# A two-model transformer forward pass on one core: the activations of all weight products move 16 bytes in SBUF

## The chip, the cores and the metric

The kernel runs on one core of a Trainium2 chip. The metric is the device time of one execution in microseconds (us), the median of a few runs. Three runs of the kernel before gave 2869.03, 2871.64 and 2883.26 us.

## The reference

Two small transformers run one after the other on a sequence of 256 tokens of 1024 features, in float32. The first has two layers of feed-forward, a mixer with four branches (a causal convolution, a short convolution, sliding-window attention, forgetting attention) and another feed-forward. The second has four layers of a mixer (differential attention, a gated recurrence, a gated unit, differential attention again), an attention over a memory of 256 tokens, and a feed-forward. Cut to what matters here:

```python
def _swiglu(x, w_gate, w_up, w_down):
    return (jax.nn.silu(x @ w_gate) * (x @ w_up)) @ w_down

for l in range(DEPTH):                       # DEPTH = 2
    x = x + 0.5 * _swiglu(_rmsnorm(x, ffn1_norm[l]), ...)
    z = _rmsnorm(x, mix_norm[l]) @ w_in[l]   # 1024 -> 6660 columns
    ...                                      # four branches, each @ its own 256 x 1024 matrix
    x = x + merged @ w_out[l]
    x = x + 0.5 * _swiglu(_rmsnorm(x, ffn2_norm[l]), ...)
for i in range(DEPTH_2):                     # DEPTH_2 = 4
    x = x + mix
    x = x + mem_cross_attention(rmsnorm(x, norm_cross[i]), mem_n, ...)
    x = x + swiglu(rmsnorm(x, norm_ffn[i]), ffn_w_gu[i], ffn_w_down[i])
return rmsnorm(x, norm_final)
```

Nearly all arithmetic is the product of 256 tokens with weight matrices of 1024 by 1024 or by 2816.

## The kernel before

**Weights.** They are cut into units of 128 partitions by 2048 float32 values (1 MB). A ring of five slots in SBUF, `raw`, takes them in from HBM in order, issued by SyncE (line 385). ScalarE rounds each unit to the reduced form float32r as its high part `wh` (line 1113), and GpSimd writes the rest, `wl` = `raw` - `wh`, over `raw` (line 400). VectorE and ScalarE do the same with activations: `ah` and `al` for the normalized input, `gh` and `gl` for the gated values of a feed-forward, `mh` and `ml`, `oh` and `ol`, `hoh` and `hol`, `soh` and `sol` in the other stages.

**A product.** TensorE adds three matmuls for each pair of tiles, high by low, low by high and high by high (`product`, lines 454 to 456). Each has a stationary operand of 128x128 and a moving operand of 128x256. In `features` the weights are stationary and the activations move; in `tokens` it is the other way round. A unit is 16 pairs, so 48 matmuls. A feed-forward stage of 33 units is 1584 matmuls.

**Order.** The order of the work on each engine is written out by hand, and semaphores tie the engines together: a unit's slot is loaded again when TensorE has signalled `unit_done`, and TensorE waits on `low_ready` before a unit. Where a stage has small attention products or a softmax, these stand between the units on TensorE.

**Addresses.** What the change touches is where things lie in SBUF. All tensors are placed by hand, with a running offset `at[0]` per partition. `sb` places a tensor at the offset and steps it by the width rounded up to 32 bytes; `w` places one inside the work area, and these names share it, stage by stage. The weights (`raw`, `wl`, `wh`) begin at a multiple of 64 bytes, and their slots are 8192 bytes apart. After them and `x` the code skips 192 bytes, and pads the work area to the same place:

```python
at[0] += 192
acts_at = at[0]
...
at[0] += (raw_at + 192 - at[0]) % 256
work_at = at[0]
```

So `ah`, `al`, `full`, `mh`, `ml` and all high and low parts in the work area start 192 bytes, modulo 256, after the start of the weights. Within each tensor a product's slice begins at a multiple of 512 bytes. `decays` (a part of the constants `con`) is multiplied with `lh` and `ll` in lines 934 and 935; they start at the same place modulo 256. `ident`, the identity that transposes use, is the first part of `con`, and lies there too, as do `vc` (keys and values of the memory), `pt2` and `prob2`.

Of the kernel before, what the change touches and what calls it, by code (L numbers as in the profile page):

```python
# [18 lines left out]
F32 = mybir.dt.float32  # L19
F32R = mybir.dt.float32r  # L20
# [5 lines left out]
P = 128  # L26
T = 256
TB = T // P
D = 1024
KD = D // P  # L30
# [98 lines left out]
def build(nc, w_units, params_d, consts_d, hot_d, rel_d, x_d, mem_d, ws_d, bs_d, out_d,  # L129
          table_d, units=UNITS, stop_after=None):  # L130

    at = [nc.sbuf_base]

    def sb(name, width, dt=F32, offset=None):

        if offset is None:
            offset = at[0]
            at[0] += (4 * width + 31) // 32 * 32
        return nc.alloc_sbuf_tensor_at(name, [P, width], dt, offset=offset)

    at[0] = (at[0] + 63) // 64 * 64
    raw_at = at[0]
    raw = sb("raw", RING * UW)
    wl = sb("wl", RING * UW, F32R, offset=at[0] - 4 * RING * UW)
    wh = sb("wh", RING * UW, F32R)
    x = sb("x", KD * T)
    at[0] += 192
    acts_at = at[0]
    ah = sb("ah", KD * T, F32R)
    al = sb("al", KD * T, F32R)  # L150
    full = sb("full", KD * T)
    mh = sb("mh", KD * T, F32R)
    ml = sb("ml", KD * T, F32R)
    par = sb("par", NPAR)
    con_at = at[0]
    con = sb("con", NCONST)
# [5 lines left out]
    at[0] += (raw_at + 192 - at[0]) % 256  # L162
    work_at = at[0]
    WORK = 12288
    work = sb("work", WORK)
    assert at[0] <= nc.sbuf_usable_end, (at[0], nc.sbuf_usable_end)

    def w(name, first, width, dt=F32):
        assert first + width <= WORK
        return sb(name, width, dt, offset=work_at + 4 * first)  # L170

    gh = w("gh", 0, FP * 512, F32R)
    gl = w("gl", FP * 512, FP * 512, F32R)

    up = w("up", 0, 2 * (CK - 1 + T))
    acc = w("acc", 576, 512)
    sp = w("sp", 1088, 2 * (SK - 1 + T))
# [2706 lines left out]
def program(nc, arrays, **kw):  # L2884
    args = [nc.dram_tensor(k, list(a.shape), F32, kind="ExternalInput").ap() for k, a in arrays.items()]
    args.append(nc.dram_tensor("out", [P, KD * T], F32, kind="ExternalOutput").ap())
    args.append(nc.dram_tensor("tables", [12, P, PERIOD], F32, kind="Internal").ap())
    build(nc, *args, **kw)
# [12 lines left out]
```

How the kernel before makes its waits and increments, by code:

```python
        @block.sync  # L365
# [8 lines left out]
                sp.dma_start(raw[:, n * UW:(n + 1) * UW], w_units[n, :, :]).then_inc(raw_landed[n], 16)  # L374
                if n == 1:
                    sp.dma_start(onehot[0:NB + 1, :], hot_d).then_inc(tables_in, 16)
                    sp.dma_start(rel[0:NB + 1, 0:12], rel_d).then_inc(tables_in, 16)
            sp.dma_start(par[:, KD:NPAR], params_d[:, KD:NPAR]).then_inc(par_rest, 16)
            sp.dma_start(con[:, :], consts_d).then_inc(consts_in, 16)
            with sp.Fori(1, units // RING) as i:
                for j in range(RING):
                    sp.wait_ge(unit_done, RING * i + (j + 1 - RING))
                    sp.dma_start(raw[:, j * UW:(j + 1) * UW], w_units[i * RING + j, :, :])\
                        .then_inc(raw_landed[j], 16)
            for c2 in range(KD // 2):
                sp.wait_ge(result, c2 + 1)
                sp.dma_start(out_d[:, 512 * c2:512 * (c2 + 1)], full[:, 512 * c2:512 * (c2 + 1)])\
                    .then_inc(stored, 16)
            sp.wait_ge(stored, 16 * (KD // 2))
# [2 lines left out]
        @block.gpsimd  # L395
# [1 line left out]
            def low(n, j):  # L397
                pool.wait_ge(high_ready, n + 1)
                pool.tensor_tensor(wl[:, j * UW:(j + 1) * UW], raw[:, j * UW:(j + 1) * UW],
                                   wh[:, j * UW:(j + 1) * UW].bitcast(F32), ALU.subtract)\
                    .then_inc(low_ready, 1)
            pool.wait_ge(low_ready, 2)
            for j in range(2, RING):
                low(j, j)
```

## Time and profile before

| what | value |
|---|---|
| runs | 2869.03, 2871.64, 2883.26 us; median 2871.64 |
| profiled execution, span | 2878.8 us (7.2 us above the median, inside the runs' range) |
| TensorE busy | 2822.3 us, 98% of the span |
| ScalarE, VectorE, GpSimd busy | 46%, 37%, 73% |
| weights moved | 459 loads of 1 MB and 4 of 256 KB |
| mean granted TensorE clock | 0.989 |

The profiled execution's own time is given by its span, from the first to the last instruction. Busy time of TensorE is no measure of its pace: matmuls are pipelined, so one is still under way when the next begins. Its pace is the distance between starts. The granted clock is the share of TensorE's full 2.4 GHz; 0.5 is the lower level of 1.2 GHz.

### The profile page before, as it was taken

Reading aid. Unit: us, or ns where it says so; the run is one execution under the profiler, and the core shown is the slowest. Engines: PE = TensorE matmul, PEld = TensorE weight load, DVE = VectorE, ACT = ScalarE, POOL = GpSimd, SP = SyncE. Lnnn points to the kernel's source line nnn. Section 1 sums busy time; section 2 is a strip of 40 time slices with the busy share of each in tenths; the row PEclk is TensorE's granted clock in tenths of the full one; section 3 lists DMA queues with packets and bytes.
Section 4 is the critical chain, followed back from the end, with each engine's and each line's share of the span. In section 5 each row is a group of like instructions: output and inputs, shape, how many; then the busy total and the mean of one; then the engine's idle time right before and its main releaser. Section 6 shows DMA issues by size and latency. Waiting matters only on the chain.

```text
span 2878.8 us, 55910 instructions
## 1 busy us (share of the span) xinstructions
PE 2822.3 (98%) x24180; PEld 2771.7 (96%) x24180; DVE 1066.5 (37%) x1865; ACT 1333.4 (46%) x1490; POOL 2108.9 (73%) x462
## 2 busy tenths in 40 slices
PE   8999999999999999999999999999999999999998
PEld 8999889999999899999999998999999999999998
DVE  4217534213155443445333144333123331453331
ACT  5335544344355454345443484444354443454442
POOL 6777657878876578776768783659886688767785
PEclk9999999999999899999999999999999999999999
DMA  7974344555554355554445542445554455544553
GB/s 231 193 198 170 135 144 176 191 185 188 199 184 152 112 192 189 182 185 147 168 169 191 191 177 87 158 144 197 191 204 153 147 195 196 191 147 161 176 192 116
DMA packets 74197, 496.88 MB, mean 173 GB/s; under 512 B 8399, under 2 KB 13135, under 8 KB 14968
## 3 DMA queue, kind: packets, MB, share of 16 engines
q1 hardware_dynamic: 68344, 485.88, 46.9%
q10 hardware_dynamic: 5632, 7.62, 2.7%
q8 instruction: 191, 3.13, 0.4%
q14 instruction: 30, 0.25, 0.0%
HBM read 490.05 MB, written 3.41 MB: 171 GB/s over the span
## 4 chain that ended last, share of the span: by engine, by line
PE 86%; POOL 4%; DMA 3%; issue 3%; DVE 2%; ACT 2%; ACTq 0%; SPq 0%; POOLq 0%; DVEq 0%
PE G L454 21%; PE G L456 21%; PE G L455 21%; PE S L454 5%; PE S L456 5%; PE S L455 5%; POOL wl L400 4%; DMA raw<-w_units 2%; PE G L691 1%; PE S L1042 1%; ACT wh L1113 1%; DMA bias<-tables 0%; PE S L842 0%; PE S L799 0%; PE S L805 0%
## 5 line engine op out<-in xcount | busy, mean ns | idle before, releaser
L400 POOL TENSOR_TENSOR wl<-raw,wh 128x2048 fp32r<-128x2048 f32 x458 | 2108.7, 4616 | 740.5 <-ACT wh L1113 719.0
L1113 ACT ACTIVATE wh<-raw 128x2048 fp32r<-128x2048 f32 x456 | 873.7, 1918 | 1045.6 <-DMA raw<-w_units 1045.5
L454 PE MATMUL G<-ah,wl 128*128 128x256 f32 x4304 | 1209.2, 281 | 15.6 <-DVE wl L1768 8.9
L455 PE MATMUL G<-al,wh 128*128 128x256 f32 x4304 | 1200.6, 279 | 0.0
L456 PE MATMUL G<-ah,wh 128*128 128x256 f32 x4304 | 1200.3, 279 | 0.0
L454 PEld LDWEIGHTS G<-ah,wl 128*128 128x128 f32 x4304 | 816.4, 190 | 24.1 <-issue 15.1
L455 PEld LDWEIGHTS G<-al,wh 128*128 128x128 f32 x4304 | 815.2, 189 | 0.6
L456 PEld LDWEIGHTS G<-ah,wh 128*128 128x128 f32 x4304 | 814.1, 189 | 0.0
L454 PE MATMUL S<-gh,wl 128*128 128x256 f32 x1408 | 391.4, 278 | 3.4 <-POOL wl L400 3.4
L455 PE MATMUL S<-gl,wh 128*128 128x256 f32 x1408 | 391.3, 278 | 0.0
L456 PE MATMUL S<-gh,wh 128*128 128x256 f32 x1408 | 391.2, 278 | 0.0
L454 PEld LDWEIGHTS S<-gh,wl 128*128 128x128 f32 x1408 | 265.0, 188 | 3.7 <-issue 3.7
L456 PEld LDWEIGHTS S<-gh,wh 128*128 128x128 f32 x1408 | 265.1, 188 | 0.0
L455 PEld LDWEIGHTS S<-gl,wh 128*128 128x128 f32 x1408 | 265.1, 188 | 0.0
L1921 DVE TENSOR_TENSOR G<-G,root 128x512 f32<-128x512 f32 x88 | 61.5, 698 | 361.3 <-PE G L456 361.3
L1959 DVE SCALAR_TENSOR_TENSOR S<-S,x 128x512 f32<-128x512 f32 x28 | 19.6, 700 | 367.1 <-PE S L456 365.9
L1919 DVE TENSOR_TENSOR G<-G,root 128x512 f32<-128x512 f32 x88 | 61.4, 698 | 184.4 <-PE G L456 184.1
L454 PE MATMUL G<-mh,wl 128*128 128x256 f32 x384 | 108.3, 282 | 3.3 <-DVE ml L2120 2.8
L454 PE MATMUL G<-wh,al 128*128 128x256 f32 x384 | 108.0, 281 | 0.8 <-DVE ll L2563 0.8
L455 PE MATMUL G<-wl,ah 128*128 128x256 f32 x384 | 107.2, 279 | 0.0
L456 PE MATMUL G<-wh,ah 128*128 128x256 f32 x384 | 107.1, 279 | 0.0
L456 PE MATMUL G<-mh,wh 128*128 128x256 f32 x384 | 106.9, 279 | 0.0
(371 smaller groups left out, 3786.3 us busy)
## 6 DMA issues: line engine op xcount, KB each, us to landing
raw<-w_units SPq DMA_DIRECT2D x459, 1024.0 KB, 4.8
bias<-tables ACTq DMA_DIRECT2D x24, 128.0 KB, 3.2
tables<-trow ACTq DMA_DIRECT2D x12, 192.0 KB, 9.0
con<-consts SPq DMA_DIRECT2D x1, 1056.0 KB, 16.8
x<-x_in SPq DMA_DIRECT2D x4, 256.0 KB, 5.8
raw<-w_units SPq DMA_DIRECT2D x4, 256.0 KB, 6.9
memx<-mem_in ACTq DMA_DIRECT2D x1, 1024.0 KB, 7.4
out<-full SPq DMA_DIRECT2D x4, 256.0 KB, 2.5
```

Of the source, the lines that this page charges most:

```text
L400: pool.tensor_tensor(wl[:, j * UW:(j + 1) * UW], raw[:, j * UW:(j + 1) * UW], wh[:, j * UW:(j + 1) * UW].bitcast(F32), ALU.subtract)\
L454: pe.matmul(out, sl, vh, start=start and k == 0, stop=False, **kw)
L455: pe.matmul(out, sh, vl, start=False, stop=False, **kw)
L456: ins = pe.matmul(out, sh, vh, start=False, stop=stop and k == len(parts) - 1, **kw)
L691: ins = pe.matmul(out, v_of(kc), pt[:, kc * 512 + n * P:kc * 512 + (n + 1) * P], start=kc == 0, stop=kc == nk // P - 1)
L1042: ins = pe.matmul(out[:, h * T:(h + 1) * T], qf[:, f * T + g * P:f * T + (g + 1) * P], kc[:, f * T:(f + 1) * T], start=dc == 0, stop=dc == 1)
L1113: act.activation(wh[:, j * UW:(j + 1) * UW], raw[:, j * UW:(j + 1) * UW], ACT.Copy)\
L1919: dve.tensor_tensor(pairs(gate), pairs(gate), along, ALU.mult).then_inc(scaled, 1)
L1921: dve.tensor_tensor(pairs(value), pairs(value), along, ALU.mult).then_inc(up_scaled, 1)
L1959: dve.scalar_tensor_tensor(xs if last else held[k], held[k], factor, xs, ALU.mult, ALU.add)\
```

## The change

Activations that enter products with weights get a helper of their own, `behind`. It places a tensor that is 4 values (16 bytes) wider at the old offset and returns the part behind these 4 values. `ah`, `al`, `full`, `mh`, `ml` and everything that `w` places in the work area now start 16 bytes further. The parameters and constants (`par`, `con` with `ident` and `decays`, `ones`, `root`, `small`) start 32 bytes further; the work area's own start stays, because the padding before it takes this up, and `merged`, `pb`, `kc`, `vc`, `memx`, `memn` and `comp` behind it start 32 bytes further. `decayed` stays. The weights and `x` stay. No instruction, wait or transfer is added, removed or put elsewhere in the order of its engine.

Modulo 256, the distance from weights to activations goes from 192 to 208. The distance from `lh` to `decays` goes from 0 to 16, that from `pt2` to `vc` and from `prob2` to `ident` too.

```diff
@@ -138,19 +138,28 @@
+    def behind(name, width, dt=F32, offset=None):
+
+        if offset is None:
+            offset = at[0]
+            at[0] += 4 * width
+        return nc.alloc_sbuf_tensor_at(name, [P, SKEW + width], dt, offset=offset)[:, SKEW:SKEW + width]
+
     at[0] = (at[0] + 63) // 64 * 64
     raw_at = at[0]
+    SKEW = 4
...
     at[0] += 192
     acts_at = at[0]
-    ah = sb("ah", KD * T, F32R)
-    al = sb("al", KD * T, F32R)
-    full = sb("full", KD * T)
-    mh = sb("mh", KD * T, F32R)
-    ml = sb("ml", KD * T, F32R)
+    ah = behind("ah", KD * T, F32R)
+    al = behind("al", KD * T, F32R)
+    full = behind("full", KD * T)
+    mh = behind("mh", KD * T, F32R)
+    ml = behind("ml", KD * T, F32R)
+    at[0] += 32
     par = sb("par", NPAR)
...
-    work = sb("work", WORK)
+    work = sb("work", WORK + 2 * SKEW)
...
     def w(name, first, width, dt=F32):
         assert first + width <= WORK
-        return sb(name, width, dt, offset=work_at + 4 * first)
+        return behind(name, width, dt, offset=work_at + 4 * first)
```

## Rows read from the trace of the kernel before

**Rows 1.** page: busy time of each engine; the chain that ended last, by engine

```profile
PE 2822.3 (98%) x24180; PEld 2771.7 (96%) x24180; DVE 1066.5 (37%) x1865; ACT 1333.4 (46%) x1490; POOL 2108.9 (73%) x462
...
PE 86%; POOL 4%; DMA 3%; issue 3%; DVE 2%; ACT 2%; ACTq 0%; SPq 0%; POOLq 0%; DVEq 0%
```

**Rows 2.** groups by line and shape: count | busy us, mean ns | idle before

```profile
L400 POOL TENSOR_TENSOR wl<-raw,wh 128x2048 fp32r<-128x2048 f32 x458 | 2108.7, 4616 | 740.5 <-ACT wh L1113 719.0 <-ACT wh L1142 20.9
L454 PE MATMUL G<-ah,wl 128*128 128x256 f32 x4304 | 1209.2, 281 | 15.6 <-DVE wl L1768 8.9 <-DVE wl L1800 3.4 <-DVE merged L2178 3.2
...
L1113 ACT ACTIVATE wh<-raw 128x2048 fp32r<-128x2048 f32 x456 | 873.7, 1918 | 1045.6 <-DMA raw<-w_units 1045.5
...
L454 PE MATMUL S<-gh,wl 128*128 128x256 f32 x1408 | 391.4, 278 | 3.4 <-POOL wl L400 3.4
...
L454 PE MATMUL G<-mh,wl 128*128 128x256 f32 x384 | 108.3, 282 | 3.3 <-DVE ml L2120 2.8 <-DVE logf L2655 0.5
L454 PE MATMUL G<-wh,al 128*128 128x256 f32 x384 | 108.0, 281 | 0.8 <-DVE ll L2563 0.8
...
L454 PE MATMUL G<-oh,wl 128*128 128x256 f32 x384 | 106.5, 277 | 0.0
...
L454 PE MATMUL G<-wh,ml 128*128 128x256 f32 x256 | 72.2, 282 | 0.0
...
L454 PE MATMUL S<-mh,wl 128*128 128x256 f32 x128 | 35.9, 280 | 1.5 <-issue 1.5
...
L454 PE MATMUL G<-soh,wl 128*128 128x256 f32 x64 | 19.5, 304 | 4.2 <-ACT kc L1238 4.2
...
L454 PE MATMUL G<-hoh,wl 128*128 128x256 f32 x64 | 17.8, 278 | 0.0
```

**Rows 3.** slower stretches: us A:B, length, PE busy (matmuls), granted clock, DMA share, GB/s

```profile
36.30:176.80 140.50, 140.50 (x1196) 1.00 0.90 201
...
463.70:646.60 182.90, 182.90 (x1555) 1.00 0.52 186
...
1720.50:1742.50 22.00, 22.00 (x189) 1.00 0.47 168
...
sum 854.40, PE 854.40; mean PE 38.84
```

**Rows 4.** faster stretches, the same view

```profile
1480.30:1658.60 178.30, 178.30 (x1576) 1.00 0.55 195
...
2697.30:2864.60 167.30, 167.30 (x1479) 1.00 0.48 170
sum 1266.70, PE 1266.70; mean PE 74.51
```

**Rows 5.** TensorE in order of time: start us, us, instruction, out<-moving,stationary

```profile
1742.68 0.29 PE L934 MATMUL S<-decays,lh 128*128 128x256 f32 x1
...
1744.36 0.28 PE L934 MATMUL S<-decays,lh 128*128 128x256 f32 x1
```

**Rows 6.** the same view, merged rows of float32 matmuls

```profile
1436.34 1.47 PE L1054 MATMUL G<-con,prob 128*128 128x128 f32 x12
...
1438.67 7.31 PE L691 MATMUL G<-pt,vc 128*128 128x128 f32 x64
```

**Rows 7.** line 2044, the convolution: duration ns min/median/max, starts, forms

```profile
L2044 DVE SCALAR_TENSOR_TENSOR S<-up,par,S x116: 480/485/493, 233.7 to 884.4; 128x256 f32<-128x256 f32 x116
```

**Rows 8.** page: loads of bias; chain of waits: start us, us, what

```profile
bias<-tables ACTq DMA_DIRECT2D x24, 128.0 KB, 3.2
...
1260.57 7.92 DMA bias<-tables
...
2481.02 6.29 DMA bias<-tables
```

## Prediction

> **What bounds the kernel now.** I read the page's shares first. TensorE is busy for 98% of the span and holds 86% of the chain that ended last; every other engine stands far below [rows 1]. Then the groups of instructions: the sums of the products with weights stand in lines 454 to 456, three matmuls for each pair of operands (low weights by high activations, high by low, high by high). Line 454 alone has 4304 + 1408 + 384 + 384 + 384 + 256 + 128 + 64 + 64 = 7376 of them [rows 2]. Times three that is 22128 products of 128x128 by 128x256, out of 24180 matmuls. The column of mean durations (some 280 ns) is no help, because matmuls overlap. What counts is the spacing from start to start, so the third view is the table by stretches: time of a stretch divided by the matmuls in it.
>
> That table shows something that no mean shows. In any long stretch without a wait the products come at one of two spacings. In 22 stretches, 854.4 us together, it is 117.8 ns: 182.9 us for 1555 matmuls gives 117.6, and 140.5 for 1196 gives 117.5 (one more start than gaps at an edge; at the third decimal it is 117.8) [rows 3]. In 17 others, 1266.7 us together, it is 113.3 ns: 178.3 us for 1576 and 167.3 for 1479 give 113.1 [rows 4]. The granted clock is 1.00 in all of them, the upper level of 2.4 GHz, so the clock is not what differs. Nor is it the work: 463.7 to 646.6 and 1480.3 to 1658.6 are the same kind of stage, a feed-forward of 1584 products, and the first takes about 4.6 us more for it. The spacing is set when the stage begins and then stays. 256 columns at 2.4 GHz are 106.7 ns, so each product loses 6.6 or 11.1 ns.
>
> What could take it? In the stream, the load of the next stationary operand runs beside the matmul, so two reads of SBUF run together: 1024 bytes per partition of the moving operand and 512 of the stationary one. All slices in the products are multiples of 512 bytes within their tensors, so each pair stands at one distance modulo 256: activations less weights is 192. Where the activations are the stationary operand it is 64 the other way round; the stretch from 1720.5 us is of that kind and has 117.8 ns too [rows 3]. One pair of the program stands at distance 0, `decays` and `lh`: there the steady spacing is 1.68 us for 14 gaps, from 1742.68 to 1744.36, or 120.0 ns [rows 5]. So the distance matters, or at least the three spacings differ with it at one clock; 0 is the worst seen, and 192 sits between two states. Other matmuls, of 128 columns and plain float32, come closer: 12 transposes in 1.47 us are (1.47 - 0.27) / 11 = 109.1 ns apart, and 64 of `pt` by `vc` in 7.31 us are 111.7 [rows 6]. They are not the same operation, and serve as a lower bound only.
>
> **The change, part by part.** No instruction is added, removed or moved on any engine; waits and queues are the same. Only addresses change.
>
> - Products by the 192 distance go to 208, those the other way round from 64 to 48. This is the only term that can be large: each nanosecond on 22128 products is 22 us. The trace has no row at 208. The nearest rows bound it: from above 120.0 ns (distance 0) [rows 5], from below 109.1 ns (the nearest matmul that keeps its full rate) [rows 6]. The present time in these terms: the slow stretches hold 854.4 / 0.1178 = 7253 products, the fast ones 1266.7 / 0.1133 = 11180; 3695 are left in short stretches, and split alike (39% slow) they make it 8700 slow and 13430 fast. The value I take is 113.3 ns for all. Two steady spacings at one distance look to me like a place at the edge of a good region, where one more or one less clash of the two reads fits into a product; 16 bytes can move it inside. That saves 8700 x 4.45 ns = 39 us. The other side is as simple: out of the region, everything at 117.8 costs 13430 x 4.45 = 60 us, everything at 120.0 costs 13430 x 6.67 + 8700 x 2.2 = 109 us.
> - `decays` by `lh` and `ll` (128 matmuls) goes from 0 to 16 bytes, since the constants move 32 and the others 16. Between 109.1 and 120.0 ns for 128 of them it is at most 1.4 us of gain, and I take 0. The float32 products of the attention (`pt`, `vc`, `prob` by the identity) go from 0 to 16 bytes apart. Besides the 22128 products and these 128 there are 1924 matmuls of all kinds, so 5 ns on each (more than the step between the two kinds in [rows 6]) would be 10 us either way. I take 0.
> - VectorE, ScalarE and GpSimd now read and write from 16 bytes past a multiple of 64. The row of the convolution's taps shows VectorE indifferent: `up` is read at 30 starting points 4 bytes apart, and 116 instructions take 480 to 493 ns [rows 7]. I take 0. ScalarE and GpSimd have no such row; both have idle time (46% and 73% busy) [rows 1], GpSimd's work on the weights lies between tensors that don't move, and a unit of 48 products at 113.3 ns (5.44 us) still covers its 4.62 us and ScalarE's 1.92 us [rows 2]. Even at 109.1 ns the unit is 5.24 us, so neither becomes the bound.
> - DMAs into `bias1`, `bias2`, `swt` and `sbs`, and those out of `full`, now start at 16 bytes past a multiple of 32. 24 loads of bias take 3.2 us at the median, and the longest pieces of the chain hold two of them, 7.92 and 6.29 us [rows 8]. If these two doubled it would be 14 us; a gain has no reason. I take 0, and 14 for the upper end.
>
> The sum: 2878.8 - 39 = 2839.8 us against the profiled execution. That span is 7.2 us above the runs' median of 2871.64, and inside their range (2869.03 to 2883.26), so the forecast for the median is 2833 us, or 1.3% less.
>
> At one place a rule speaks against this. The Trainium skill, page "TensorE: Matmul & The Clock Gate", section on what happens when a matmul is issued, says that TensorE has two independent read ports into SBUF and that loading the next weights takes nothing from the running matmul. The same page, in the section on 56 against 53.3 ns, gives 2.5 ns over the columns' time, which would be 109.2 ns here. By that the distance could not matter. The rows don't fit it: 113.3, 117.8 and 120.0 ns at one clock. But if the port rule holds and the spacing comes from something else that is set at a stage's start, the change does nothing but deal the spacings anew; that is the second rival.
>
> **The rivals.**
>
> 1. Toward the bad distance. 208 is nearer to 256, and 48 nearer to 0, than 192 and 64 were, and 0 is where 120.0 ns stands. The price is that of one more stall in each product: all at 117.8 ns gives 2872 + 60 = 2932 us, all at 120.0 gives 2981. It decides from the point where the mean spacing passes 115.1 ns, today's mean ((8700 x 117.8 + 13430 x 113.3) / 22130). For it: the only measured point on that side is the worst one, and the two read streams drift past each other once in each 256 bytes, so a step of 16 may just as well add a meeting. Against it: 16 bytes of 64 is a short way, and the state at 113.3 ns already holds most of the time.
> 2. Nothing but a new deal. The distance is not what sets the spacing, or 208 has the same two states. The state taken on by a single feed-forward stage is worth 1584 x 4.45 ns = 7 us, and the runs' own range is 14 us wide; the sum then lies within 2872 +- 14 us. For it: the same distance shows both spacings in the same kind of stage. Against it: distance 0 has a third spacing that neither stretch shows.
> 3. Clear of it altogether. All products at 111.7 ns would give 2833 - 22128 x 1.6 ns = 2798 us, at 109.1 ns 2740 us. For it: other matmuls do this in the same program [rows 6]. Against it: those have half the columns, and no product with weights has been seen there at all.
>
> **How the numbers follow.** The forecast has 0.36, the first rival 0.33, the second 0.19, the third 0.12. The likeliest case's own range is 2815 to 2855 us. Cases of both signs hold most of the chance, so the whole range must reach into both: 2775 us leaves out the deeper half of the third rival, 2940 takes in the 117.8 ns state and leaves out a part of the way to 120.0 ns. A change of under 0.5% (14 us) is one that a measurement of this kernel can hardly tell from none. Faster by more than that: 0.36 + 0.12, less 0.03 for a smaller gain, plus 0.03 of the new deal, 0.48. Slower: 0.33 plus 0.02 of the new deal, 0.35. Within it, 0.17.
>
> **What would show it.** Right: the table by stretches gives 113.3 ns (1584 products of a feed-forward in about 179.5 us) also where it gave 117.8, the feed-forward stage from 463.7 us first of all; the chain keeps its shape, and the durations of VectorE, ScalarE, GpSimd and the loads of bias are what they were. Wrong in its first step: the two spacings stand side by side as before. Wrong in its sign: 117.8 or 120.0 ns in stretches that had 113.3. If a gain comes with spacings unchanged, or the float32 matmuls or the bias loads account for more than 10 us of the difference, my cause is wrong even where the time is right.

## The result and the profile after

The changed kernel takes 2957.24 us (median of 4 runs, 2951.71 to 2962.39) against 2870.34 us before (2868.42 to 2883.26). The ratio is 1.0288 with an interval of 1.0258 to 1.0317: 2.9% slower. The forecast was 2833 us, with a range of 2775 to 2940 us, so both the sign and the upper end were wrong. In two of the runs further down, one execution was far from the others of its kernel (3112.94 us at distance 64, at a mean granted clock of 0.845, and 6928.81 us with the constants alone); the medians leave these two out.

The page of the kernel after, busy time of each engine, the chain by engine, and the two groups that ride beside the products (lines have moved by 9):

```profile
span 2955.5 us, 55910 instructions
PE 2903.0 (98%) x24180; PEld 2852.0 (96%) x24180; DVE 1065.3 (36%) x1865; ACT 1333.2 (45%) x1490; POOL 2108.9 (71%) x462
...
PE 87%; POOL 3%; issue 3%; DMA 3%; DVE 2%; ACT 2%; ACTq 0%; SPq 0%; POOLq 0%; DVEq 0%
...
L409 POOL TENSOR_TENSOR wl<-raw,wh 128x2048 fp32r<-128x2048 f32 x458 | 2108.7, 4616 | 815.7 <-ACT wh L1122 794.1
L1122 ACT ACTIVATE wh<-raw 128x2048 fp32r<-128x2048 f32 x456 | 873.1, 1917 | 1100.8 <-DMA raw<-w_units 1100.4
...
bias<-tables ACTq DMA_DIRECT2D x24, 128.0 KB, 3.3
```

Nothing but TensorE has changed. GpSimd's and ScalarE's busy times are those of [rows 1, 2] to 0.2 us, and they only wait longer (815.7 against 740.5 us). The loads of bias take 3.3 against 3.2 us. VectorE's taps, from the changed start, are as quick as in [rows 7] (min/median/max in ns):

```profile
L2053 DVE SCALAR_TENSOR_TENSOR S<-up,par,S x116: 480/487/491, 234.2 to 900.8; 128x256 f32<-128x256 f32 x116
```

The table by stretches is where the time lies. TensorE of the kernel after: stretch, its length, busy time with the matmuls in it, granted clock, DMA share, GB/s. One matmul takes some 0.28 us and the next starts 0.12 us after it, so two that began earlier are counted in each window; the spacing is the length over the count less two. (By that, the rows before give 117.8 and 113.3 ns to the digit: 182.9 / 1553 and 178.3 / 1574. The count can be one off at an edge, so a short window is good to 1 ns only.)

```profile
36.00:178.00 142.00, 142.00 (x1194) 1.00 0.89 198
471.30:656.10 184.80, 184.80 (x1553) 1.00 0.52 184
661.30:845.40 184.10, 184.10 (x1581) 1.00 0.54 191
...
1507.00:1695.00 188.00, 188.00 (x1580) 1.00 0.52 185
...
2765.00:2941.40 176.40, 176.40 (x1483) 1.00 0.45 162
```

The first, second, fourth and fifth stand at 119.1 to 119.2 ns, the third at 116.6. There is no stretch at 113.3 left. These are products of the 208 distance. The 1920 products with the activations stationary went from distance 64 to 48, and they became a little quicker, from 117.8 ns [rows 3] to 116.7 over their starts (116.4 by the row):

```profile
1731.40:1753.40 22.00, 22.00 (x191) 1.00 0.56 191
```
The feed-forward stage that took 178.3 us for 1576 matmuls [rows 4] now takes 188.0 for 1580, at the same clock. Read one by one, the starts do not step evenly. The same view as in [rows 5], in the stretch that ends some 4 us before that stage and stands at 119.2 ns too:

```profile
1499.75 0.28 PE L465 MATMUL G<-ah,wh 128*128 128x256 f32 x1
1499.87 0.28 PE L463 MATMUL G<-ah,wl 128*128 128x256 f32 x1
1499.99 0.29 PE L464 MATMUL G<-al,wh 128*128 128x256 f32 x1
1500.12 0.28 PE L465 MATMUL G<-ah,wh 128*128 128x256 f32 x1
```

In nanoseconds the gaps repeat 119, 118, 118, 120, 124, 121, 119, 114: eight in 953, or 119.1. What to see is steps of 0.11 to 0.13 us in a pattern that repeats; the stage after it shows the same one.

Taken over all starts in both traces, the gaps of under 135 ns between neighbouring products (21,803 before, 21,784 after; the rest stand at waits or at the lower clock) have a mean of 115.07 ns before and 118.69 after. Their sum goes from 2508.8 to 2585.6 us, and everything outside them is 370.0 and 369.9 us. The span grew by 76.7 us, so the products are all of it.

### The profile page after: what moved, and what is told of

Same layout as the page of the kernel before. It is cut to its first block, busy times and chain, and to the rows that moved or that the text cites. A ratio compares the mean times of both kernels' runs of the same rounds, so it can differ in the third digit from the quotient of the medians.

```text
span 2955.5 us, 55910 instructions
## 1 busy us (share of the span) xinstructions
PE 2903.0 (98%) x24180; PEld 2852.0 (96%) x24180; DVE 1065.3 (36%) x1865; ACT 1333.2 (45%) x1490; POOL 2108.9 (71%) x462
## 4 chain that ended last, share of the span: by engine, by line
PE 87%; POOL 3%; issue 3%; DMA 3%; DVE 2%; ACT 2%; ACTq 0%; SPq 0%; POOLq 0%; DVEq 0%
PE G L463 21%; PE G L465 21%; PE G L464 21%; PE S L463 5%; PE S L465 5%; PE S L464 5%; POOL wl L409 3%; DMA raw<-w_units 3%; PE G L700 1%; PE S L1051 1%; ACT wh L1122 1%; DMA bias<-tables 1%; PE S L851 0%; PE S L808 0%; PE G L874 0%
## 5 line engine op out<-in xcount | busy, mean ns | idle before, releaser
L409 POOL TENSOR_TENSOR wl<-raw,wh 128x2048 fp32r<-128x2048 f32 x458 | 2108.7, 4616 | 815.7 <-ACT wh L1122 794.1
L463 PE MATMUL G<-ah,wl 128*128 128x256 f32 x4304 | 1229.2, 286 | 14.4 <-DVE wl L1777 9.3
L464 PE MATMUL G<-al,wh 128*128 128x256 f32 x4304 | 1220.9, 284 | 0.0
L465 PE MATMUL G<-ah,wh 128*128 128x256 f32 x4304 | 1220.3, 284 | 0.0
L463 PE MATMUL S<-gh,wl 128*128 128x256 f32 x1408 | 397.4, 282 | 2.2 <-POOL wl L409 2.2
L464 PE MATMUL S<-gl,wh 128*128 128x256 f32 x1408 | 397.3, 282 | 0.0
L465 PE MATMUL S<-gh,wh 128*128 128x256 f32 x1408 | 397.3, 282 | 0.0
L463 PE MATMUL G<-oh,wl 128*128 128x256 f32 x384 | 109.0, 284 | 0.0
L465 PE MATMUL G<-oh,wh 128*128 128x256 f32 x384 | 108.5, 283 | 0.0
L464 PE MATMUL G<-ol,wh 128*128 128x256 f32 x384 | 108.5, 283 | 0.0
```

The costliest lines, as they stand in the source:

```text
L409: pool.tensor_tensor(wl[:, j * UW:(j + 1) * UW], raw[:, j * UW:(j + 1) * UW], wh[:, j * UW:(j + 1) * UW].bitcast(F32), ALU.subtract)\
L463: pe.matmul(out, sl, vh, start=start and k == 0, stop=False, **kw)
L464: pe.matmul(out, sh, vl, start=False, stop=False, **kw)
L465: ins = pe.matmul(out, sh, vh, start=False, stop=stop and k == len(parts) - 1, **kw)
```

## The experiments

**The distance, measured by itself.** A small kernel with only the disputed matmuls; `s` is the block's step in values, and the two `fc` and eight `k` of three units give 144 products a block:

```diff
+STEPS = [4 * n for n in range(64)]
+UNITS = 3
...
+                            a = k * 256 + fc * P
+                            b = s + k * 256
...
+                            pe.matmul(o, wl[:, a:a + P], ah[:, b:b + 256], start=first and fc == 0, stop=False,
+                                      skip_group_check=True)
+                            pe.matmul(o, wh[:, a:a + P], al[:, b:b + 256], start=False, stop=False,
+                                      skip_group_check=True)
+                            ins = pe.matmul(o, wh[:, a:a + P], ah[:, b:b + 256], start=False, stop=last,
+                                            skip_group_check=True)
```

> A kernel that holds only the disputed matmuls: 64 blocks of 144 products (three for each pair of operands, stationary 128x128, moving 128x256, float32r, as in the big kernel), in each block the moving operand starts 4 bytes further from the stationary one modulo 256 (0, 4, ... 252). It leaves everything else of the computation out. Distance theory (the spacing of products depends on the distance modulo 256 between the two operands): the block at 192 shows 113.3 or 117.8 ns, the one at 208 119.2, the one at 0 120.0, and there is a smooth or stepped curve between. Alignment theory (an operand that starts off a multiple of 32 bytes is read more slowly, whatever stands beside it): all blocks at multiples of 32 bytes (0, 32, ... 224) are alike at 113 to 118 ns, all others are slower.

TensorE in six of the blocks, windows of 90 gaps (columns as above): distances 0, 64, 112, 176, 192 and 208.

```profile
21.57:32.37 10.80, 10.80 (x92) 1.00 0.01 2
313.89:324.09 10.20, 10.20 (x92) 1.00 0.01 2
533.50:543.71 10.21, 10.21 (x92) 1.00 0.00 0
...
826.85:837.58 10.73, 10.73 (x92) 1.00 0.00 0
900.08:910.67 10.59, 10.59 (x92) 1.00 0.01 2
973.33:984.06 10.73, 10.73 (x92) 1.00 0.00 0
```

120.0, 113.3, 113.4, 119.2, 117.7 and 119.2 ns. The small kernel gives back the big one's numbers: 119.2 at 208, 117.8 at 192, 120.0 at 0. The alignment theory is out, since 128 (118.7) and 160 (118.7), multiples of 32, are slow and 112 is not. The curve is not smooth either. At the places between multiples of 16 it jumps about between 116.9 and 123.3, and of all 64 places only 64 and 112 reached 113.3 (192 stood at its slower value).

**Both operands 16 bytes on.** The changed kernel with the weights moved too:

```diff
-    raw = sb("raw", RING * UW)
-    wl = sb("wl", RING * UW, F32R, offset=at[0] - 4 * RING * UW)
-    wh = sb("wh", RING * UW, F32R)
+    raw = behind("raw", RING * UW)
+    wl = behind("wl", RING * UW, F32R, offset=at[0] - 4 * RING * UW)
+    wh = behind("wh", RING * UW, F32R)
+    at[0] += 32
     x = sb("x", KD * T)
-    at[0] += 192
+    at[0] += 160
```

> The changed kernel, but the weights (raw, wl, wh) are placed 16 bytes further too, so every weight product stands at a distance of 192 again while both operands start 16 bytes off a multiple of 32. Distance theory: spacings of 113.3 and 117.8 ns return, time within 1% of the kernel before (2842 to 2899 us). Alignment theory: at least as slow as the changed kernel, 2957 us or more.

2852.86 us; ratio to before 0.9905 (0.9876 to 0.9934). Activations and constants lie exactly as in the changed kernel; only the weights differ, by 16 bytes (and `x`, which enters no product with these weights, by 32). That is worth 104 us between the two medians, each from its own series. So the activations' addresses alone are not the cause: it takes the weights' place too. Its feed-forward stages stand at 113.3 ns:

```profile
458.50:634.50 176.00, 176.00 (x1555) 1.00 0.55 194
1458.50:1637.40 178.90, 178.90 (x1581) 1.00 0.54 195
```

In this profile no stretch of products at distance 192 stands at 117.8 ns; only those at 64, with the activations stationary, are slower (mostly 118.3). One thing besides TensorE changed. GpSimd now works between weights that start 16 bytes off, and each of its instructions takes 0.6% longer, 4645 against 4616 ns [rows 2] (4647 in a second profile). It still has room:

```profile
L410 POOL TENSOR_TENSOR wl<-raw,wh 128x2048 fp32r<-128x2048 f32 x458 | 2121.2, 4645 | 702.0 <-ACT wh L1123 680.2
```

**The other direction, and the farthest place.**

```diff
-    at[0] += 192
+    at[0] += 160        # with SKEW = 4: 176;  for 128: += 128 with SKEW = 0
...
-    at[0] += (raw_at + 192 - at[0]) % 256
+    at[0] += (raw_at + 160 - at[0]) % 256
```

> The mirror of the change: activations at 176 bytes modulo 256 from the weights, 16 below 192 instead of 16 above. Alignment theory: as slow as at 208, 2957 us. Distance theory: the spacing is that of the curve at 176 and, for products the other way round, at 80, one value in all long stretches; if it gets better with distance from 0, 113.3 ns or less, and 2835 us or less.

> Activations at 128 bytes modulo 256 from the weights, the farthest from 0, and all tensors at multiples of 32 bytes. If nearness to 0 alone is what costs, this is the best place: 113.3 ns or less everywhere, 2835 us or less. Alignment theory: like the kernel before, 2870 us.

176: 2962.36 us, ratio 1.0289 (1.0249 to 1.0328). 128: 2958.15 us, 1.0267 (1.0225 to 1.0308). Both are as slow as 208. Rows of feed-forward stages, 176 first (the stage that took 188.0 us above), then two earlier stages of 128:

```profile
1510.00:1698.20 188.20, 188.20 (x1580) 1.00 0.52 185
```

```profile
466.30:652.70 186.40, 186.40 (x1555) 1.00 0.51 183
657.70:845.10 187.40, 187.40 (x1582) 1.00 0.52 187
```

That is 119.3 at 176, and 120.0 and 118.6 at 128. So the nearness to 0 is not what costs: the place farthest from it is as bad as the changed kernel. 192 is a narrow good place with worse ones 16 bytes away on both sides.

**Two other good places.** By the curve, 64 and 112.

> Activations at 64 bytes modulo 256 from the weights (constants move with them, all at multiples of 32 bytes). Distance theory with the measured curve: products with stationary weights at 64 stand at 113.3 ns always, those the other way round (1920 of 22128) at 192, so at 113.3 or 117.8; mean 113.4 to 113.8 against 115.07 before, 28 to 37 us less: 2835 to 2850 us. If the place or the entry decides more than the distance: the mixture of 113.3 and 117.8 of the kernel before, 2855 to 2890 us.

> Activations at 112 bytes modulo 256 from the weights, 16 bytes off a multiple of 32. The curve has 113.3 ns at 112 and 116.7 at 144, where the products the other way round come to stand: mean about 113.6 ns, 2840 us. Anything near the changed kernel's 2957 us would say that the curve of the small kernel doesn't carry over.

```diff
-    at[0] += 192
+    at[0] += 64         # with SKEW = 0; for 112: += 96 with SKEW = 4
...
-    at[0] += (raw_at + 192 - at[0]) % 256
+    at[0] += (raw_at + 64 - at[0]) % 256
```

64: 2926.21 us, 1.0174 (1.0134 to 1.0215), a miss: 76 us above the forecast, and above the range of the other branch as well. 112: 2858.27 us, 0.9943 (0.9916 to 0.9971), near the forecast of 2840 though 18 us above it. The rows of one stage each, 64 first:

```profile
1493.40:1679.20 185.80, 185.80 (x1580) 1.00 0.52 187
```

```profile
1458.50:1637.40 178.90, 178.90 (x1581) 1.00 0.55 195
```

At 64 all long stretches stood at 117.7 ns, at 112 at 113.4. The curve had shown only one of the spacings that 64 can have. The trace of the kernel before held the other: its products with stationary activations are at distance 64, and the stretch of them from 1720.5 us stands at 117.8 [rows 3].

**Start places and entries.** The start place is where the stationary operand begins modulo 256; an entry is the point after a wait at which a block or stage starts its stream. The small kernel with both operands moved together:

```diff
-STEPS = [4 * n for n in range(64)]
+STEPS = [(d, b) for d in (192, 64, 112, 192) for b in range(0, 256, 16)]
+STEPS = [(d, b) for b in (0, 16, 64, 80) for d in range(0, 256, 16)]      # the second of the two kernels
```

> Only the disputed matmuls again, 64 blocks of 144 products: the distance is 192, 64, 112 and again 192 bytes, and at each both operands move together through the start places 0, 16, ... 240 modulo 256. Everything else of the computation is left out. If only the distance counts: the blocks at 64 and 112 stand at 113.3 ns at every start place, those at 192 at 113.3 or 117.8 ns, dealt in a way that has nothing to do with the place. If the place counts too (the kernel with both operands 16 bytes on was 0.95% faster than before, all its feed-forward stages at 113.4): at 192 the block at some places is 113.3 in both passes, at others 117.8 in both.

> Only the disputed matmuls: 64 blocks of 144 products, 16 distances (0, 16, ... 240) at each of four start places (0, 16, 64, 80), so that every distance is entered four times in different ways; everything else is left out. If each distance has its own set of steady spacings and the entry picks one of them: 208, 176 and 128 never show 113.3 ns, and 64, 112 and 192 show it at least once among 117.8 to 120.0. If the entry alone decides and any distance can have any spacing: 208 shows 113.3 in one or two of its four blocks, and the difference between before and after is one of luck at the entry.

In the first, 192 stood at 113.3 ns in 31 of 32 blocks and at 117.8 in one; 64 had 113.3, 117.8 and 118.3; 112 had 113.3 at all multiples of 32 and 120.0 (once 116.7) at the places between. The second gave, in ns for start places 0, 16, 64, 80 (mean of the last 96 gaps of each block):

```
distance    0: 120.0 118.3 120.0 118.3      128: 118.7 120.0 118.7 120.0
           16: 118.7 117.3 113.3 117.4      144: 118.6 120.0 118.6 119.9
           32: 116.7 118.3 116.7 118.3      160: 117.3 116.7 117.3 117.8
           48: 118.3 116.7 118.3 116.7      176: 119.3 118.7 119.3 118.8
           64: 117.8 113.3 117.8 113.3      192: 113.3 113.3 113.3 113.3
           80: 120.0 118.1 120.0 118.1      208: 119.2 117.8 119.2 117.8
           96: 120.0 120.0 120.0 120.0      224: 118.3 120.0 118.3 120.0
          112: 113.3 118.3 113.3 120.0      240: 117.1 118.3 117.2 118.3
```

The blocks of distance 208, in order of start place, and the one of distance 16 at start place 64:

```profile
256.73:267.46 10.73, 10.73 (x92) 1.00 0.01 2
545.84:556.44 10.60, 10.60 (x92) 1.00 0.01 2
834.97:845.70 10.73, 10.73 (x92) 1.00 0.01 2
1124.51:1135.11 10.60, 10.60 (x92) 1.00 0.01 2
...
618.91:629.11 10.20, 10.20 (x92) 1.00 0.01 2
```

208 has 119.2 and 117.8 ns and never 113.3, as 176 and 128 have not; 64, 112 and 192 have it, and so has 16, once in four blocks. Start places 64 bytes apart give nearly the same column (16 is the exception), those 16 apart another one. So, as far as these blocks go, each distance has its own set of steady spacings, and start place and entry pick from it. The products with stationary activations in the full kernels fit these blocks. Over the starts they stand at 118.3 ns with both operands on (distance 64, start place 208; 118.3 in the first small kernel there), at 118.1 in the kernel of 176 (distance 80; 118.1 in the second at start place 16), and at 120.0 in that of 112 (distance 144; 120.0 there).

**What is held up.** Other shapes at 16 distances each:

```diff
-STEPS = [4 * n for n in range(64)]
+STEPS = [(d, v) for v in ((64, 256), (128, 512), (128, 128)) for d in range(0, 256, 16)]
+STEPS = [(d, v) for v in ((4, 256), (32, 256), (96, 256)) for d in range(0, 256, 16)]      # the second kernel
...
-                            pe.matmul(o, wl[:, a:a + P], ah[:, b:b + 256], start=first and fc == 0, stop=False,
+                            pe.matmul(o, wl[:, a:a + cols], ah[:, b:b + width], start=first and fc == 0, stop=False,
```

> Only such matmuls, everything else left out: 16 distances (0, 16, ... 240 bytes) in each of three shapes. Load theory (the clash holds up the load of the next stationary operand, and a product waits for its load): with a moving operand of 512 columns the load has time to spare, so the spacing is the same 215 to 217 ns at all distances; with a stationary operand of 64 columns the load is half as long, so some 109 ns at all distances; with 128 moving columns the load alone sets 107 to 120 ns, and it varies. Stream theory (the clash holds up the moving operand as well): the spacing varies with the distance at 512 columns too, by as much again or more as at 256.

> Only such matmuls, everything else left out: 16 distances with a stationary operand of 4, of 32 and of 96 columns, moving operand of 256 columns. If what holds up the stream is the load of the stationary operand that runs beside it: at 4 columns 109 to 110 ns at every distance, at 32 columns one or two nanoseconds more, at 96 nearly the full loss and its dependence on the distance. If the stream of 256 columns has a spacing of its own that owes nothing to loads: 113.3 ns or more at 4 columns too.

Distances 192 and 208 with 64 stationary columns, 0, 192 and 208 with 512 moving ones, and 192 and 208 with 128 moving ones:

```profile
232.21:242.92 10.71, 10.71 (x92) 1.00 0.00 0
250.04:260.54 10.50, 10.50 (x92) 1.00 0.01 2
307.77:328.17 20.40, 20.40 (x91) 1.00 0.00 1
721.11:742.11 21.00, 21.00 (x91) 1.00 0.00 0
755.88:777.00 21.12, 21.12 (x91) 1.00 0.00 1
1055.70:1065.76 10.06, 10.06 (x92) 1.00 0.00 0
1072.45:1082.50 10.05, 10.05 (x92) 1.00 0.01 2
```

With 128 columns every distance gives 111.7 ns, so a full load of 128 columns fits into that time. With 512 columns it has twice as much, and still the spacing is 226.7 to 236.7 ns and varies with the distance. The load theory falls: a product does not wait for a late load, the stream beside the load is held up. What inside it is, no run shows. The order of the distances is that of one shape only: with 64 stationary columns 192 (119.1 ns) is slower than 208 (116.7), and with 512 moving ones 0 is one of the two quickest of the 16. In the second kernel, distances 64 and 192 with 4 stationary columns, then 192 with 32, then 64 and 192 with 96:

```profile
89.55:99.75 10.20, 10.20 (x92) 1.00 0.00 0
226.17:236.37 10.20, 10.20 (x92) 1.00 0.00 0
...
504.10:514.30 10.20, 10.20 (x92) 1.00 0.00 0
...
644.07:654.66 10.59, 10.59 (x92) 1.00 0.00 0
786.39:796.89 10.50, 10.50 (x92) 1.00 0.00 0
```

With loads of 4 columns 14 of 16 distances stand at 113.3 ns and two (0 and 224) at 116.7. With 32 and 96 columns the spread over the distances is back, up to 120.0. So 113.3 ns is what the moving stream of 256 float32r columns needs with hardly a load beside it, and no block of 256 columns was quicker. Nearly all above it comes with the loads, and depends on the distance. The 109 ns that my expectation had for 4 columns was seen at no distance.

**Parts of the change.** Only the work area on, and only parameters and constants on (step 0):

```diff
-    ah = behind("ah", KD * T, F32R)           # first kernel; al, full, mh, ml in the same way
+    ah = sb("ah", KD * T, F32R)
...
-    SKEW = 4                                  # second kernel
+    SKEW = 0
```

> One part of the change alone: only the tensors of the work area (gh, gl, oh, ol, hoh, hol, soh, sol, lh, ll and the plain ones) start 16 bytes further; ah, al, full, mh and ml stay at 192. Distance theory: the 4224 products of gh and gl and 1536 of oh, ol, hoh, hol, soh and sol go to 119.2 ns, the others keep 113.3 or 117.8: 5760 x (119.2 - 115.1) = 24 us more than before, 2895 us, with the deal of the others 2880 to 2915. If all tensors of the change must be 16 bytes on to be slow: 2871 us.

> The change with a step of 0 instead of 4 values: activations stay at 192, only parameters and constants start 32 bytes further. If the loss is in the products with weights: 2871 us +- 14, spacings of 113.3 and 117.8. If moving the constants had a share (ident by prob, decays by lh): it shows here alone, 5 us or more in the stages with attention and in the gated recurrence.

> The same kernel as in the run with constants alone, which took 24 us more than before with activations still at 192, and whose profile was of a disturbed execution. If the loss is a deal of spacings at the entries of stages: the table by stretches shows only 113.3 and 117.8 ns for the products, with about 24 / 0.00445 = 5400 products more at 117.8 than before, and the rest of the kernel (float32 matmuls, waits) the same to 3 us. If the constants' place costs by itself: the products' mean is 115.1 as before and the rest is 24 us longer.

Work area alone: 2914.96 us, 1.0136 (1.0097 to 1.0174), 20 us above the forecast. Constants alone: 2896.64 us, 1.0078 (1.0046 to 1.0111), and again 2899.91 us, 1.0099 (1.0082 to 1.0115). That one I had not expected: with every activation still at 192 it is 24 and 29 us slower. In the profile of the second run the stages stand like this:

```profile
458.30:641.20 182.90, 182.90 (x1556) 1.00 0.52 186
1478.80:1664.60 185.80, 185.80 (x1580) 1.00 0.53 187
1147.70:1261.40 113.70, 113.70 (x1005) 1.00 0.54 196
```

117.7, 117.7 and 113.4 ns: no third spacing, but a deal with more of the slow one (the deal: which of its spacings each stage takes). The mean of the gaps is 115.86 ns, which on all products is 17 us more than in the first profile of before, of the 22 us by which the span is longer. Most of the other 5 us is the clock: 228 pairs of neighbouring products start some 213 ns apart, the pace of the lower level of 1.2 GHz, against 189 before. One place where only this profile has it, its row and that of before:

```profile
172.00:178.50 6.50, 5.26 (x25) 0.50 0.36 140
172.00:178.50 6.50, 5.42 (x47) 1.00 0.91 386
```

Why tensors that enter none of these products change the deal is not shown. With the work area alone, a feed-forward is split as foreseen, its part with `ah` (192) and its part with `gh` (208):

```profile
470.00:570.00 100.00, 100.00 (x852) 1.00 0.52 185
595.00:640.00 45.00, 45.00 (x381) 1.00 0.48 173
```

100.0 / 850 is 117.6 and 45.0 / 379 is 118.7 (119.2 over all 4210 gaps of `gh`). The tensors at 208 have 208's spacing and the others one of 192's, in one stage of one kernel. That is the most direct evidence that the distance decides, since execution and clock are the same for both parts, and in the kernel before both parts of that stage stand at 117.8 ns. This kernel also contains the move of the constants, which my expectation forgot: from their 2896.64 us in the same series the work area adds 18.

**Is the deal fixed?** The kernel before once more, and the version with both operands 16 bytes on.

> The kernel before, once more, for its stretches. If an entry's outcome is fixed by the program and addresses: the same stretches stand at 117.8 ns as in the first profile, and the time is within 5 us of it. If it is dealt anew in each execution: some feed-forward stages have changed sides, each worth 7 us.

> The version with both operands 16 bytes on, distance 192, once more, as the candidate that beats both kernels. If its gain is a property of where the operands lie: 0.985 to 0.995 of before again, and every feed-forward stage at 113.4 ns. If it was a lucky deal: anywhere from 0.99 to 1.01, with stretches at 117.8 ns.

Before again: 2867.98 us, span 2866.1. The first two of these stretches had changed sides, the other two had not:

```profile
36.50:170.00 133.50, 133.50 (x1180) 1.00 0.89 203
459.60:635.50 175.90, 175.90 (x1554) 1.00 0.55 193
1465.90:1644.80 178.90, 178.90 (x1581) 1.00 0.55 195
1129.90:1248.10 118.20, 118.20 (x1006) 1.00 0.53 190
```

The two stood at 117.8 ns in the first profile [rows 3] and have 113.3 now. From 1130 us on the five stretches of more than 1000 products are as they were. The mean of all products went from 115.07 to 114.51 ns, 12 us, and the span fell by 12.7. So the deal differs in part between executions, and in part was the same in both profiles. It is large enough for the 15 us between the runs of one kernel, but only two executions were profiled, and the mean granted clock varies from run to run too (0.986 to 0.992 over the runs of the kernel before).

Both operands on, again: 2852.88 us against 2871.08, ratio 0.9942 (0.9928 to 0.9956), with the means 113.85 ns in the first profile and 113.80 in the second. It has the lowest time here (the kernel of 112 comes within 6 us) and is quicker than the kernel before in both series.

## Why the prediction was wrong

**The bound was read rightly.** TensorE's products with weights set the time, their spacing and not their count changes, and the other terms were all near nothing: VectorE, ScalarE, GpSimd, the loads of bias and the float32 matmuls together moved the time outside the products by 0.1 us. `decays` by `lh` too had no weight. One reading was off. The 4.6 us between the two feed-forward stages compare windows of 1555 and 1576 products; on the 1584 of a whole stage it is the 7 us of the second rival.

**The step that failed** is the value taken for the 22128 products: "The value I take is 113.3 ns for all", with the reason that two steady spacings look "like a place at the edge of a good region" and "16 bytes can move it inside". The runs showed 119.2 ns (118.69 in the mean), so the term came out as a cost of 77 us and not as a gain of 39. The reason is false. There is no region: 192 is one good value, 176 and 208 at its sides are 2.9% slower, and the curve jumps with every 4 bytes. Two spacings at one distance do not mark an edge either, since 64 has three and 208 has three (119.2, 117.8 and, in one feed-forward stage of the big kernel, 116.6). The spacings at 192 say nothing about those at 208. The trace before held one value at another distance, 120.0 ns at 0 [rows 5], and I gave it less weight than the picture of the edge.

**The first rival** had the right sign and nearly the right size: it priced 117.8 ns at 2932 us and 120.0 at 2981, and 2957 lies between. Its mechanism is not what the runs show. It said that nearness to 0 is what costs; 176, farther from 0, and 128, the farthest, cost as much. No run shows that the two reads meet once in each 256 bytes.

**The second rival**, a new deal of spacings, is real but another thing: it moved the same kernel by 12 us, and the kernel with moved constants by 17. It could not give 77: every product at 117.8 ns would be 60, and 208 was never seen at 113.3 ns.

**The third rival** is excluded: 113.3 ns is reached with hardly any load beside the stream and was passed in no block of 256 columns, so 111.7 or 109.1 were not to be had by a move. They came from other shapes [rows 6], as its own text said; 128 moving columns have 111.7 at every distance.

**The base of the count.** The 39 us that I saw as a gain were there, and the version with both operands on took most of them: 113.8 ns instead of 115.07 is 28 us in the spans' terms. The gain was at the old distance, not at the new one. In both profiles of that version every stretch at 192 has 113.3 ns, while with the weights at a multiple of 64 both spacings occur in every profile; the small kernel, with 192 at 113.3 in 31 of 32 blocks, doesn't show why.

**The range.** Its upper end of 2940 us left out the part of the way to 120.0 ns, though the only measured point on that side was 120.0. The bound from the row was 2981, and a range that kept it would have held the time.

What stays open: why 64, 112 and 192 (and once 16) have the undisturbed spacing and their neighbours have not, what picks a state at the entry, and why moving the constants changes the deal. The pattern, its persistence and its dependence on both operands' places are shown; a mechanism inside the chip is not.

## What to carry to other kernels

Where a stream of matmuls sets the time, read its spacing from start to start, stage by stage. Two values at one clock and one kind of work are a reason to test the place of the operands. Then measure the distances in a small kernel with several entries and start places for each, since the neighbours of a good value say nothing, and with the shape that the kernel uses, since another shape orders them differently. Then time each layout in the full kernel, with a second profile: a harmless looking step of one operand cost 2.9%, the same step for both gained 0.6 and 0.95%, and moving only tensors outside these products cost 0.8 and 1%.

## What the runs showed of the hardware

- A stream of float32r products of 256 moving columns has a spacing of 113.3 ns at a granted clock of 1.00 with loads of only 4 columns beside it (14 of 16 distances). With 512 columns it has 226.7 ns at the least. Both are 0.443 ns a column.
- Full loads of 128 columns add 0 to 10 ns at 256 columns (113.3 to 123.3), by the distance of the two operands modulo 256, and 0 to 10 ns at 512 columns. The Trainium skill, page "TensorE: Matmul & The Clock Gate", section on what happens when a matmul is issued, says that loading the next weights takes no SBUF read bandwidth from the running matmul. By that the size of the load should not matter to the stream. The traces disagree (at distance 208, 113.3 ns with loads of 4 columns and 119.2 with 128), and the measurement decides; that read bandwidth is what is lost, no run shows.
- At one distance several steady patterns exist (192: 113.3 and 117.8 ns; 208: 116.6, 117.8 and 119.2). A feed-forward stage of 1584 products at one distance kept its pattern to the end, and which it takes can differ between executions.
- VectorE's taps (480 to 491 against 480 to 493 ns) and the loads of bias (3.3 against 3.2 us) took the same time from 16 bytes past a multiple of 32. GpSimd's tensors did not move in the changed kernel. Where they did, with both operands on, its instruction took 4645 ns against 4616.
